# Convolution as 32-column products over stacked shifts, memory heads in pairs, and chunk quarters in other steps of the last mixer

## The reference, cut to what matters

```
a, gate = split(hn @ a_w_in[..., :1536])
h = a * sigmoid(gate)                                    # 768 channels, 256 tokens
y[t, c] = sum over j in 0..30 of w[j, c] * h[t - 30 + j, c]  + bias[c]
primary = silu(layer_norm(y))                            # over the 768 channels
q_mem   = rms_norm(hn @ a_w_in[..., 1536:], per head of 64)
mem_out = softmax(q_mem @ k_mem / 8) @ v_mem             # 4 heads of 64, 256 memory rows
x = x + concat([primary, mem_out]) @ w_o[0]
```

## Time and profile before

| | us |
|---|---|
| median of the 3 runs | 1742.2 (1741.06 to 1742.25) |
| the profiled execution: its own time | 1738.93 |
| span in its trace | 1737.1 |
| PE busy in the span | 1609.9 (93%) |
| DVE busy | 961.8 (55%) |
| ACT busy | 712.9 (41%) |
| POOL busy | 15.8 (1%) |
| mean granted TensorE clock | 0.984 |

### The profile page before, as it was taken

How to read it: one execution, slowest core, us unless ns; L and a number is a source line. 1 busy time by engine, 2 the same in 40 slices (tenths; PEclk the granted TensorE clock), 3 DMA queues, 4 the chain that set the end, 5 groups by cost and what they waited for, 6 DMA issues and landing times.

```text
span 1737.1 us, 30364 instructions
## 1 busy us (share of the span) xinstructions
PE 1609.9 (93%) x12395; PEld 1302.6 (75%) x12407; DVE 961.8 (55%) x1677; ACT 712.9 (41%) x1108; POOL 15.8 (1%) x31
## 2 busy tenths in 40 slices
PE   7999999887878888999999999999999999799999
PEld 6988866555545554788879778888788888678887
DVE  4886451111101110667668967676767677557666
ACT  5455451001101100545455665445545454554443
POOL 2000000000000000000000000000000000000000
PEclk9999999999999899999999999999999999899999
DMA  9644479999999999765555035554465554135560
GB/s 302 231 165 147 158 306 428 428 429 429 429 428 428 428 428 418 241 217 176 187 169 173 23 98 181 204 190 172 145 217 172 191 173 143 49 122 191 172 217 25
DMA packets 162878, 409.53 MB, mean 236 GB/s; under 512 B 5367, under 2 KB 127374, under 8 KB 150524
## 3 DMA queue, kind: packets, MB, share of 16 engines
q1 hardware_dynamic: 160944, 404.54, 62.3%
q0 software_dynamic: 1632, 4.01, 0.8%
q10 hardware_dynamic: 236, 0.06, 0.0%
HBM read 407.54 MB, written 1.05 MB: 235 GB/s over the span
## 4 chain that ended last, share of the span: by engine, by line
PE 68%; DMA 20%; DVE 6%; ACT 4%; issue 1%; SPq 0%; ACTq 0%; DVEq 0%
PE bank L1205 18%; DMA odd_expert<-in_w_up_dram 15%; PE bank L579 9%; PE bank L580 9%; PE bank L581 9%; PE bank L1209 9%; DMA odd_expert<-in_w_gate_dram 5%; PE bank L969 3%; PE bank L1186 2%; DVE wlo L1915 1%; PE bank L994 1%; ACT whi L1415 1%; DVE x L1953 1%; PE bank L762 1%; PE bank L736 1%
## 5 line engine op out<-in xcount | busy, mean ns | idle before, releaser
L1205 PE MATMUL bank<-x,whi 128*128 128x512 f32 x1408 | 356.3, 393 | 1.2 <-DVE x L1953 0.9
L1205 PEld LDWEIGHTS bank<-x,whi 128*128 128x128 f32 x1408 | 255.8, 189 | 50.9 <-issue 2.0
L2454 DVE TENSOR_TENSOR wlo<-raw,whi 128x2048 fp32r<-128x2048 f32 x120 | 271.4, 2289 | 32.6 <-ACT whi L1733 27.2
L1733 ACT ACTIVATE whi<-raw 128x2048 fp32r<-128x2048 f32 x120 | 225.4, 1913 | 57.9 <-PE bank L581 57.9
L1209 PEld LDWEIGHTS bank<-x,wlo 128*128 128x128 f32 x1408 | 193.7, 190 | 13.5
L1209 PE MATMUL bank<-x,wlo 128*128 128x256 f32 x1408 | 200.8, 282 | 0.0
L1915 DVE TENSOR_TENSOR wlo<-raw,whi 128x2048 fp32r<-128x2048 f32 x67 | 152.8, 2289 | 67.9 <-ACT whi L1415 67.2
L1415 ACT ACTIVATE whi<-raw 128x2048 fp32r<-128x2048 f32 x67 | 126.9, 1909 | 40.0 <-PE bank L581 35.3
L579 PE MATMUL bank<-whi,hh_hi 128*128 128x512 f32 x352 | 138.1, 392 | 3.1 <-DVE hh_lo L2439 3.0
L580 PE MATMUL bank<-whi,hh_lo 128*128 128x512 f32 x352 | 137.5, 391 | 0.0
L581 PE MATMUL bank<-wlo,hh_hi 128*128 128x512 f32 x352 | 137.0, 389 | 0.0
(11 more groups left out here) (343 smaller groups left out, 2376.5 us busy)
## 6 DMA issues: line engine op xcount, KB each, us to landing
raw<-in_ffn_w_gate_dram SPq DMA_DIRECT2D x44, 1024.0 KB, 5.5
raw<-in_ffn_w_up_dram SPq DMA_DIRECT2D x44, 1024.0 KB, 6.9
raw<-in_ffn_w_down_dram SPq DMA_DIRECT2D x44, 1024.0 KB, 6.6
raw<-in_w_gate_dram SPq DMA_DIRECT2D x16, 2048.0 KB, 21.5
raw<-in_w_up_dram SPq DMA_DIRECT2D x16, 2048.0 KB, 24.7
raw<-in_w_down_dram SPq DMA_DIRECT2D x16, 2048.0 KB, 24.9
odd_expert<-in_w_gate_dram SPq DMA_DIRECT2D x16, 2048.0 KB, 26.3
odd_expert<-in_w_up_dram SPq DMA_DIRECT2D x16, 2048.0 KB, 26.3
```

The source lines that it names most:

```text
L1205: pe.matmul(bank[:, :], hi[:, k, :], x_both[x][:, k, :, :].rearrange("p b n -> p (b n)"), start=k == 0, stop=False, skip_group_check=True)
L1733: act.activation(whi[:, c0_ % SPLIT, :], raw[:, c0_ % RAW, :], ACT.Copy).then_inc(hi_ready, 1)
L2454: dve.tensor_tensor(wlo[:, c0_ % SPLIT, :], raw[:, c0_ % RAW, :], whi[:, c0_ % SPLIT, :].bitcast(F32), ALU.subtract).then_inc(lo_ready, 1)
```

## The change

**The convolution.** It goes wholly to PE. For each tile of 128 channels, SP copies `conv_in` within the on-chip memory into `stacked`: for each block of 32 channels, four copies stand above each other in the 128 partitions, shifted by 0, 8, 16 and 24 positions (16 DMAs for each tile, `stack_tile`). POOL multiplies a stack of four 32x32 identities by the weights (`kernels`, one instruction for each tile). PE then needs, for each block of 32 channels, 8 products of 128 rows by 32 columns, where product `s` takes the taps `s`, `s+8`, `s+16`, `s+24` at once: 32 products for each tile, 192 in all. `stacked` and `kernels` have two buffers each, so that the copies and the build for tile `ct` wait until the products of tile `ct - 2` are done (`conv_done`). The taps on DVE, the diagonals on ACT, and two bank clears go away. DVE adds the bias while it takes the tiles out of their banks (`conv_rows`).

**The memory heads.** The four heads of the first mixer go two at a time, with the functions of the last mixer.

**The output product** of the first mixer starts only when the sum of the squares is done and its result written (`cms_ready`); before, half of its first chunk stood ahead of that sum.

**The last mixer.** The quarters and ACT's and DVE's chunk work stand in other steps.

**The start.** The weights' two DMAs become four, with runs of 32 values; `in_taps` counts 12 in place of 10.

```diff
+            def stack_tile(ct):
+
+                sp.wait_ge(glu_done, ct // 2 + 1)
+                if ct >= 2:
+                    sp.wait_ge(conv_done, ct - 1)
+                for i in range(BLOCKS):
+                    for shift in range(BLOCKS):
+                        sp.dma_start(stacked[ct % 2][32 * shift:32 * shift + 32, i, :],
+                                     conv_in[32 * i:32 * i + 32, ct, SHIFTS * shift:SHIFTS * shift + STACKW]).then_inc(
+                                         stack_in[ct % 2], 16)
...
             while c < n_chunks:
+                for ct in {conv_at + 10: (0, 1), conv_at + 14: (2, 3, 4, 5)}.get(c, ()):
+                    stack_tile(ct)
...
-            pool.dma_start(rows_b, taps[0:P]).then_inc(in_taps, 16)
-            pool.dma_start(rows_c[0:DW_ROWS - P, :], taps[P:DW_ROWS]).then_inc(in_taps, 16)
+            pool.dma_start(rows_b[:, 0:96].rearrange("r (a c) -> r a c", a=3), lead[0:P]).then_inc(in_taps, 16)
+            pool.dma_start(rows_b[:, 96:P], taps[3 * DW_ROWS:3 * DW_ROWS + P]).then_inc(in_taps, 16)
+            pool.dma_start(rows_c[0:DW_ROWS - P, 0:96].rearrange("r (a c) -> r a c", a=3), lead[P:DW_ROWS]).then_inc(in_taps, 16)
+            pool.wait_ge(zero_ready, 1)
+            last = 24 * CONV_TAPS - 3 * DW_ROWS - P
+            pool.dma_start(rows_c[0:last, 96:P], taps[3 * DW_ROWS + P:24 * CONV_TAPS]).then_inc(in_taps, 16)
...
+            for ct in range(CONV_TILES):
+                if ct >= 2:
+                    pool.wait_ge(conv_done, ct - 1)
...
+                pool.tensor_tensor(kernels[ct % 2],
+                                   cst[:, C_STACK:C_END].unsqueeze(1).unsqueeze(1).broadcast_to([P, SHIFTS, BLOCKS, 32]),
+                                   w.unsqueeze(3).broadcast_to([P, SHIFTS, BLOCKS, 32]), ALU.mult).then_inc(kernel_ready, 1)
...
+            def conv_tile(ct):
+
+                pe.wait_ge(stack_in[ct % 2], 16 * BLOCKS * BLOCKS * (ct // 2 + 1))
+                pe.wait_ge(kernel_ready, ct + 1)
+                for s in range(SHIFTS):
+                    for i in range(BLOCKS):
+                        mm = pe.matmul(conv_bank(ct)[32 * i:32 * i + 32, :], kernels[ct % 2][:, s, i, :],
+                                       stacked[ct % 2][:, i, s:s + TOK], start=s == 0, stop=s == SHIFTS - 1,
+                                       skip_group_check=True)
+                mm.then_inc(conv_done, 1)
...
+            conv_tile(0)
             head_sums()
...
-            tap_group(0)
+            conv_tile(1)
             head_scales()
-            tap_group(1)
+            conv_tile(2)
             pe.wait_ge(hn_ready, n["hs"])
+            pair_scores(pairs[0][0])
+            conv_tile(3)
+            pair_scores(pairs[1][0])
+            conv_tile(4)
+            conv_tile(5)
+            pe.wait_ge(conv_ready, 4)
+            pair_turn(FULL_BLOCKS)
             pe.wait_ge(evac_v, evac_count[c0 + 6][1])
...
-            attend([memory_head(0, head) for head in range(4)], taps_beside)
...
+            for ct in range(CONV_TILES):
+                pe.wait_ge(conv_ready, ct + 1)
+                mm = pe.matmul(linear_bank(c0 + 6)[:, 0:TOK], ones, conv_out[:, ct, :], start=ct == 0, stop=ct == CONV_TILES - 1)
+            mm.then_inc(csum_done, 1)
+            pair_values(8, pairs[0][2])
+            pair_turn(FULL_BLOCKS)
+            pair_values(10, pairs[1][2])
+            for ct in range(CONV_TILES):
+                pe.wait_ge(csq_ready, ct + 1)
+                mm = pe.matmul(linear_bank(c0 + 6)[:, TOK:2 * TOK], ones, conv_sq[:, ct, :], start=ct == 0,
+                               stop=ct == CONV_TILES - 1, skip_group_check=True)
             mm.then_inc(csum_done, 1)
             start_outer(c0 + 7)
             pe.wait_ge(o_evac, n["out"])
-            linear_outer(c0 + 7, 0, 3, 1, tts=(0,))
...
+            pe.wait_ge(cms_ready, 1)
+            linear_outer(c0 + 7, 0, 3, 1)
...
-                for at in {1: (0, 1), 2: (2, 3), 3: (4,), 4: (5,), 5: (6, 7)}.get(step, ()):
+                for at in {0: (0, 1), 1: (2, 3), 3: (4, 5), 4: (6, 7)}.get(step, ()):
                     row_quarter(c0 + 8 + at // 4, 1, at % 4)
...
             def beside_heads(step):
+                if step == 0:
+                    round_to(c0 + 11)
                 if step == 2:
-                    round_to(c0 + 11)
+                    values(1)
                 if step == 3:
-                    values(1)
+                    round_to(c0 + 12)
                 if step == 5:
-                    round_to(c0 + 12)
-                if step == 6:
                     values(2)
...
             def beside_heads(step):
                 if step == 0:
                     scaled(6, qm_t[1])
-                if step == 2:
                     split_to(c0 + 11)
-                if step == 5:
+                if step == 3:
                     split_to(c0 + 12)
```

More of the change, by code:

```diff
@@ L89 @@
 CONV_TAPS, CONV_TILES = 31, 6
-TAP_GROUPS = [(j, 4) for j in range(0, CONV_TAPS, 4)]
-PE_TAPS = 4
-TAP_GROUPS += [(j, 2) for j in range(0, PE_TAPS, 4)]
-DW_ROWS = CONV_TAPS * CONV_TILES
+SHIFTS, BLOCKS = 8, 4
+DW_ROWS = SHIFTS * CONV_TILES * BLOCKS
 G_DW, G_HEAD = 128, 128 + DW_ROWS
```

267 lines of the change are left out of this document (103 added, 164 removed).

## The result

The changed kernel takes **1749.3 us** (median of 6 runs, 1745.8 to 1749.9) against 1741.95 for the kernel before in the same comparison: ratio **1.0036, 95% interval 1.0024 to 1.0047**, so 6.3 us slower (the two medians are 7.4 apart; below I go by the ratios). The forecast was 1731.5, with 1724 to 1741 as range: wrong in sign and outside the range. The profiled execution took 1749.02, its span is 1747.2.

The account below looks back on a forecast made before the run. PE was taken as the bound, with 68% of what ended last. 6.4 us won in the first mixer plus 5.0 in the last, less 0.7 at the start, gave 10.7 below 1742.2: 1731.5, range 1724 to 1741.

Parts of the forecast that it names:

- SP's price: First mixer: SP's issue of each copy was taken as 0.38 us, with 0.32 and 0.46 as ends.
- Slower, by SP's issues: Rival, 12%: in the first mixer 0.55 us for a copy makes it even; at 0.70 the time is 1752.
- The products: First mixer: four column groups run at once on PE, so a tile takes 3.84 us and six take 23.0.
- The buffers just suffice: First mixer: a buffer's turn takes 11.7 us, against 12.2 of issuing for two tiles.
- 1.3 for half clock at one tile: First mixer: half clock after PE's waits costs 1.3 us, so tile 5 ends at 988.0.
- POOL's build is free: First mixer: POOL's weight build, at least 1.15 us, costs nothing up to 6.1 us for a tile.
- The tail: First mixer: 12.2 us from tile 5's end to the output product, which then takes 22.4.
- The last mixer, 5.0 won: Last mixer: step 7 starts 3.0 us earlier and its products avoid half clock, 2 more; between 2 and 7.
- The start, 0.7 lost: Start: POOL's two more small DMAs delay PE's first transpose by 0.7 us, between 0 and 1.5.
- 6.4 were to be won: First mixer as a whole: it ends at 1022.6 in place of 1029.05, 6.4 us won.
- SP is no bound: Rival, 13%: issues come far faster, PE's work bounds the first mixer; tile 5 ends at 981.3, time 1725.
- POOL's build: Rival, 4%: a build above 6.1 us paces tiles 2 to 5 of the first mixer; at 12, time 1755.

Follow-up runs that it names:

- both: The changed kernel with one copy for a pair of tiles and the copies shared between SP and POOL; ratio 0.9872 to the kernel before, 1719.5 us.
- after: The changed kernel itself, in its first profile, against the kernel before; ratio 1.0036, median 1749.3 us.

## Why the prediction was wrong

**The step that failed is SP's price.** The forecast says "With some hundredths between two I take 0.38, nearest to SP's many rows". Measured are 0.662, and over 64 copies that is 18.1 us more than forecast; tile 5 ends 17.8 late (1005.8 for 988.0), and 1749.3 is 17.8 above 1731.5. The rival *Slower, by SP's issues* had the mechanism, its formula gives 1731.5 + 18.1 = 1749.6, and its chance was 12%. That this meets the median to 0.3 us is luck: the same kernel's second median was 1746.3, and terms of 1 to 3 us elsewhere (half clock at tile 5, the tail, the last mixer) happened to cancel. What stood in the rows was the price of a load that SP issues alone: SP's issues in the earlier trace rows lie microseconds apart, and the one row of two behind each other gave 0.43. I took both as one kind, and "no SP row is above 0.44" as evidence against 0.55; but none of these rows was of a copy whose source and target are both on the chip, or of a long series. And that sentence, like "this trace has 0.37 for each issue", is true only of the rows that I had picked. In the trace of the kernel before, 18 of SP's 291 issues are longer, most of them where loads follow each other at once. Four such loads at the start:

```profile
L460 SPq DMA_DIRECT2D raw<-in_w_in_dram x4: 379/508/886, 11.3 to 12.8; - x4
```

The issues right behind them take up to 10.6. These are loads of 1 MB, so not the copies' case, and no run here isolates what holds them; but they were the rows of SP in a series, and they spoke against 0.46 as an upper end. The range should have reached to the 1752 that the text itself had worked out.

The rule that the prediction weighed, of the Trainium skill, "DMA: Bandwidth & Descriptors", section on the anatomy of one DMA, puts the sequencer's dispatch at about 50 ns. The runs say 0.51 for a lone copy and 0.66 in a series, on SP. The section is headed as that of GpSimd's path, which the prediction didn't say, so it never spoke of SP. On GpSimd's path an issue held POOL for 0.49; the page's 50 ns is one part of such an issue, and no run here splits it. Going by the row was right, but the row was of another case.

**The other terms, each by its row:**
- *The products.* 3.68 for a tile, 3.84 forecast; `both` has all six so.
- *The buffers just suffice.* Not put to the test: at 0.66 for a copy two tiles need 21.2 of issuing, far more than a buffer's turn of 11.7, and SP never waited for the buffers in tiles 3 to 5.
- *1.3 for half clock at one tile.* 1.4 at tile 5 in the first profile (5.05 for 3.67), 2.9 in the second; at tiles 2 to 4 it is hidden in the waits. The length of the waits, 3.8 to 6.7, was underestimated with SP's price.
- *POOL's build is free.* 1.94 against bounds of 1.15 and 6.1. By the Trainium skill, "GPSIMD Engine Reference", section on elementwise work, it was an estimated 2.25; the trace is 14% below.
- *The tail.* 11.4 for 12.2, and the output product without its waits 21.9 for 22.4, against 29.2 before.
- *The last mixer, 5.0 won.* 6.8 (4.7 to 9.1) alone, 3.3 (0.4 to 6.2) in the changed kernel; 4 to 7 in the profiles' stretches. One figure in its text is off: 24 products at half of 0.224 are 2.7 us, not 2.9; no term hangs on it.
- *The start, 0.7 lost.* 0.67 at the first product.

By these measured parts the first mixer, from the seventh chunk's end to the filler, takes 85.7 (953.4 to 1039.16) for 76.2 before: 9.5 lost where 6.4 were to be won. With 0.7 lost at the start that is 10.2, and the two profiled spans are 10.1 apart (1747.2 and 1737.1), for in that execution the last mixer gave nothing. With some 5 won there, as in the comparisons, it would be 5.2 slower; measured were 6.3.

**The rivals.** *SP is no bound* was a sound sum: `both` makes its condition true, and the time is 5 us below the 1725 that it gave. *POOL's build* above 6.1 is refuted: it took 1.94. The mechanism of the forecast was right, SP's issue paces tiles 2 to 5; one price, off by 0.28, decided the sign, because it stood in the sum 64 times with nothing to hide it.

## What to carry to other kernels

A price that is multiplied by 64 is worth more care than the rest of the sum: ask whether the rows show the same operation in the same situation (source and target, alone or in a series), look through the whole trace for the longest of its kind and not only the usual one, and if it isn't there, let the range reach to where the sign turns. The many small DMAs on the path were paid in the issuing queue here, by their number and not by their bytes. So look whether each can be made larger, and whether two queues can share them; either gave 24 us over the changed kernel, and both together 29. And one profile can show a gain as lost that the timings have, or the other way round: stretches between fixed points, compared over several kernels, told one execution's half clock from the change's effect, and a profile's own time should be held against the median before it is taken for the kernel.

## What the runs showed that I had not expected

- SP's issue of a DMA costs 0.37 for a lone weight load, 0.51 for a lone copy inside the chip, 0.56 in a series from DRAM and 0.64 to 0.76 in a series of 8 or more inside the chip, from 4 bytes to 2104 for each of 32 rows. Single ones in a series take up to 2.0. A weight load right behind the copies takes 0.58 too, and the fourth of such loads behind each other 3.53 (`after`, at 949.69).
- POOL issues such copies at 0.49 (a tile's) and 0.54 (a pair's), less than SP, and they land after 1.7 to 3.6 us, with medians of 1.9 and 2.7.
- POOL's 1.94 for a two-operand build becomes 4.00 beside DVE's two-operand split, which takes 3.07 for 2.29 in the same time. The rows of the changed kernel, of POOL and of DVE, show turns: DVE's split starts at 927.08 while POOL's first build runs until 927.97, and lasts 0.78 longer; POOL's second build starts there and lasts 2.06 longer, about as long as the split still runs (until 930.15). The Trainium skill, "SBUF — State Buffer", section on the two separate sides, says that a DVE instruction with two SBUF inputs and a GpSimd instruction that reads SBUF take a pair of ports in turns, each for its whole length; the trace agrees. In `both` a build that begins at 972.36 beside a split takes 3.36. POOL had time for it here, and PE has no wait between 925 and 953 in the changed kernel's profile, so DVE's 0.8 cost nothing.

```profile
927.97 4.00 POOL L604 TENSOR_TENSOR prob_t<-cst,cols 128x1024 f32<-128x1024 f32 x1
```

```profile
927.08 3.07 DVE L1930 TENSOR_TENSOR wlo<-raw,whi 128x2048 fp32r<-128x2048 f32 x1 [0.86 <-ACT whi L1462]
```
